# Part of the FFN down products by seven sub-products instead of eight

## The chip, the cores and the metric
One Trainium2 chip, one core. The metric is the device time of one execution in microseconds (us), the median of several runs. Engines: TensorE (PE) multiplies, ScalarE (ACT), VectorE (DVE) and GpSimd (POOL) do elementwise work, SyncE (SP) issues most transfers.

## The reference
Two transformer blocks with four SwiGLU FFNs in all, on 256 tokens of width 1024, in 32-bit floats. Each FFN computes

```
x = x + 0.5 * ((silu(h @ w_gate) * (h @ w_up)) @ w_down)     h = rmsnorm(x)
```

with a hidden width of 2816. `w_down` is 2816 x 1024. The change touches only the product with `w_down`; the rest (mixing layers, attention, norms) is as it was.

## The kernel before
Every product is made from three matmuls on values rounded to the engine's fast 32-bit form: both operands are split in a high part (rounded) and a low part (what is left), and high x high, high x low and low x high are added up in PSUM. The hidden values are split once per FFN (`hid_hi`, `hid_lo`: 22 row blocks of 128, by 256 tokens). The weights are split on the fly, granule by granule.

A granule is a 1 MB piece of weights (4 row blocks of 128 by 512 columns, here called weight blocks; a small one has 2). It goes through a ring of four slots (RING = 4), in three buffers of four slots each: `raw`, `whi`, `wlo`. For granule number g:

- SP loads it into `raw` (`load`, L275) once the low part of granule g - 4 has been made;
- ScalarE makes the high part (`split_hi`, L311), once it is loaded and TensorE has finished granule g - 4;
- VectorE (first granule of a unit) or GpSimd (second granule) makes the low part (`split_lo`, L316);
- TensorE waits for the low part and multiplies (`multiply`, `triple`, L335 to L337), then raises `gran_done`.

A unit is two granules. Each engine works through a program written out by hand, in order; an instruction that waits holds all behind it on that engine. The ring is counted through the whole kernel, so the next stage's first granules are split while the last ones of this stage are multiplied.

In the down stage of an FFN there are six units: for each half of the 1024 output columns three units, with 22 row blocks: granules of 4, 4, 4, 4, 4 and 2. Each granule serves both blocks of 128 tokens: 4 x 2 x 3 = 24 matmuls of 512 columns for a full one. The front half goes to one pair of PSUM banks, the back half to the other pair. VectorE adds each half to x, scaled by half of the token's reciprocal norm (`residual`, L471), and for the front half TensorE transposes the new x in between (`transpose_x`, L416). In the last FFN the last unit is multiplied token block by token block (`multiply_by_token`), so that the end of the kernel can begin sooner.

Before it, in the up stage, 11 units are worked through in the same ring (a loop of three turns over units 3 to 8, `TURNS`). For each piece of 128 hidden columns ScalarE evacuates a part (`low`, L661), VectorE joins (L775), scales and multiplies, ScalarE rounds (L672) and VectorE makes the rest (L789); GpSimd has one split per unit only.

## Time and profile before

| | us |
|---|---|
| median of 3 runs | 1344.33 (1344.03 to 1344.72) |
| span of the profiled execution, first to last instruction | 1343.3 |
| TensorE busy | 1335.2 |
| ScalarE busy | 759.8 |
| VectorE busy | 721.2 |
| GpSimd busy | 536.3 |

The profiled execution is given by its span; the runs are timed around it, and their median stands 1.0 us above the span. Busy time counts the records of an engine. Matmul records overlap, as the engine is pipelined: the price of a matmul on the path is the distance between two starts, not the length of its record. The mean granted TensorE clock was 0.999 of full speed.

### The profile page before, as it was taken

The page shows a single profiled execution, that of the slowest core. Times are in us where ns is not written, and L with a number is a line of the kernel's source. Part 1 is how long each engine was busy: PE and PEld are TensorE (multiplying, and loading weights), DVE is VectorE, ACT ScalarE, POOL GpSimd, SP SyncE. Part 2 cuts the span into 40 slices and gives each one's busy share as a digit, 9 for nine tenths or more (in the row PEclk, how much of TensorE's full clock was granted, in tenths as well). Part 3 has the DMA queues.
Part 4 walks back from the last instruction along what each step waited for, and adds up shares of the span by engine and source line. Part 5 has one row for each costly group of instructions (what it writes and reads, how often), then busy time and mean ns, then how long its engine had stood idle before and what let it go on. Part 6 is the DMA issues. An engine that isn't in the chain of part 4 may idle for free.

```text
span 1343.3 us, 18749 instructions
## 1 busy us (share of the span) xinstructions
PE 1335.2 (99%) x7360; PEld 1128.6 (84%) x7360; DVE 721.2 (54%) x978; ACT 759.8 (57%) x1059; POOL 536.3 (40%) x188
## 2 busy tenths in 40 slices
PE   9999999999999999999999999999999999999998
PEld 8888888888888888888888887788888888888887
DVE  6655346955555444555346659754335642555534
ACT  7655357456555446555347687667434655655533
POOL 1444343474544345444344331035525524444433
PEclk9999999999999999999999999999999999999999
DMA  9656454234655545555454655355855543655550
GB/s 340 226 188 228 172 188 157 96 111 157 212 190 190 207 162 190 197 188 175 173 188 160 240 169 192 122 183 168 300 170 179 177 168 126 208 183 187 188 188 32
DMA packets 38809, 244.32 MB, mean 182 GB/s; under 512 B 5936, under 2 KB 6480, under 8 KB 10832
## 3 DMA queue, kind: packets, MB, share of 16 engines
q1 hardware_dynamic: 36832, 235.08, 51.0%
q10 hardware_dynamic: 1904, 8.23, 1.7%
q8 instruction: 50, 0.82, 0.2%
q14 instruction: 23, 0.19, 0.0%
HBM read 242.21 MB, written 1.08 MB: 181 GB/s over the span
## 4 chain that ended last, share of the span: by engine, by line
PE 96%; DVE 1%; ACT 1%; DMA 1%; issue 0%; SPq 0%; POOLq 0%; POOL 0%; DVEq 0%; ACTq 0%
PE acc L350 21%; PE acc L335 17%; PE acc L337 16%; PE acc L336 16%; PE acc L351 12%; PE acc L353 3%; PE acc L2655 2%; PE work L1006 1%; PE acc L2656 1%; DMA raw<-in_t_ffn_up 1%; PE work L1091 1%; PE work L416 1%; PE work L1097 1%; DVE conv_out L1040 1%; PE work L1940 1%; PE work L2702 1%
## 5 line engine op out<-in xcount | busy, mean ns | idle before, releaser
L316 POOL TENSOR_TENSOR wlo<-raw,whi 128x2048 fp32r<-128x2048 f32 (+1 forms) x104 | 478.5, 4602 | 626.2 <-ACT whi L311 618.3
L311 ACT ACTIVATE whi<-raw 128x2048 fp32r<-128x2048 f32 (+1 forms) x221 | 414.4, 1885 | 98.6 <-PE acc L337 95.6
L350 PE MATMUL acc<-xT,whi 128*128 128x512 f32 x1208 | 427.9, 396 | 0.2 <-DVE work L775 0.2
L316 DVE TENSOR_TENSOR wlo<-raw,whi 128x2048 fp32r<-128x2048 f32 x117 | 298.7, 2553 | 211.9 <-ACT whi L311 211.6
L351 PE MATMUL acc<-xT,wlo 128*128 128x256 f32 x1384 | 373.7, 280 | 0.0
L350 PEld LDWEIGHTS acc<-xT,whi 128*128 128x128 f32 x1208 | 226.6, 188 | 51.0 <-DVE xT L455 0.9
L351 PEld LDWEIGHTS acc<-xT,wlo 128*128 128x128 f32 x1384 | 261.3, 189 | 7.3
L335 PE MATMUL acc<-whi,xT 128*128 128x512 f32 x416 | 168.4, 405 | 0.0
L337 PE MATMUL acc<-whi,xT 128*128 128x512 f32 x416 | 162.5, 391 | 0.0
L336 PE MATMUL acc<-wlo,xT 128*128 128x512 f32 x416 | 162.4, 390 | 0.0
L335 PE MATMUL acc<-whi,hid_hi 128*128 128x512 f32 (+1 forms) x358 | 138.3, 386 | 0.0
L337 PE MATMUL acc<-whi,hid_lo 128*128 128x512 f32 (+1 forms) x358 | 138.1, 386 | 0.0
L336 PE MATMUL acc<-wlo,hid_hi 128*128 128x512 f32 (+1 forms) x358 | 138.0, 386 | 0.0
L775 DVE TENSOR_TENSOR work<-acc,low_parts 128x512 f32<-128x512 f32 x88 | 61.6, 699 | 106.4 <-ACT low_parts L661 105.8
L661 ACT ACTIVATE low_parts<-acc 128x512 f32<-128x512 f32 x88 | 52.6, 598 | 94.2 <-PE acc L353 93.4
L335 PEld LDWEIGHTS acc<-whi,xT 128*128 128x128 f32 x416 | 78.1, 188 | 17.1 <-DVE xT L455 0.7
L337 PEld LDWEIGHTS acc<-whi,xT 128*128 128x128 f32 x416 | 78.1, 188 | 16.8
L336 PEld LDWEIGHTS acc<-wlo,xT 128*128 128x128 f32 x416 | 78.3, 188 | 14.7 <-issue 0.2
L337 PEld LDWEIGHTS acc<-whi,hid_lo 128*128 128x128 f32 x358 | 67.2, 188 | 13.5
L336 PEld LDWEIGHTS acc<-wlo,hid_hi 128*128 128x128 f32 x358 | 67.3, 188 | 13.4
L335 PEld LDWEIGHTS acc<-whi,hid_hi 128*128 128x128 f32 x358 | 67.3, 188 | 13.3
L428 ACT ACTIVATE junk<-x 128x512 bf16<-128x512 f32 (+1 forms) x33 | 20.4, 617 | 93.3 <-DVE x L471 76.1
(402 smaller groups left out, 1617.8 us busy)
## 6 DMA issues: line engine op xcount, KB each, us to landing
raw<-in_t_ffn_up SPq DMA_DIRECT2D x85, 1024.0 KB, 5.0
raw<-in_t_m_in SPq DMA_DIRECT2D x52, 1024.0 KB, 4.9
raw<-in_t_ffn_down SPq DMA_DIRECT2D x40, 1024.0 KB, 4.9
raw<-in_t_m_os SPq DMA_DIRECT2D x8, 1024.0 KB, 5.2
raw<-in_t_ffn_down SPq DMA_DIRECT2D x8, 512.0 KB, 3.5
raw<-in_t_m_out SPq DMA_DIRECT2D x4, 1024.0 KB, 4.9
sum_rows<-row_scratch ACTq DMA_DIRECT2D x4, 1024.0 KB, 4.8
raw<-in_t_m_oa SPq DMA_DIRECT2D x4, 1024.0 KB, 5.1
```

Source lines behind the costliest of these rows:

```text
L311: act.activation(granule(whi, u, i), granule(raw, u, i), ACT.Copy).then_inc(hi_ready, 1)
L316: eng.tensor_tensor(granule(wlo, u, i), granule(raw, u, i), granule(whi, u, i).bitcast(F32), ALU.subtract).then_inc(lo_odd if g % 2 else l ...
L335: pe.matmul(to, xhi[:, kt, tok], hi, start=first, stop=False)
L336: pe.matmul(to, xhi[:, kt, tok], lo, start=False, stop=False)
L337: return pe.matmul(to, xlo[:, kt, tok], hi, start=False, stop=last)
L350: pe.matmul(to, hi[:, c], both_parts(kt), start=first, stop=False)
L351: mm = pe.matmul(to[:, 0:T], lo[:, c], xT_hi[:, kt, :], start=False, stop=False)
L353: mm = pe.matmul(to, hi[:, c], both_parts(kt), start=False, stop=True)
L428: act.activation(junk[:, 0:src.shape[-1]], src, ACT.Square, accum_out=total).then_inc(squares, 1)
L661: act.activation(low_parts[m % 2][:, :, :], acc[:, 2 * q:2 * q + 2, T:2 * T], ACT.Copy).then_inc(ffn_low, 1)
L775: dve.tensor_tensor(work[:, m % 4, :].rearrange("p (a t) -> p a t", a=2), acc[:, 2 * q:2 * q + 2, 0:T], low_parts[m % 2][:, :, :], ALU.add ...
L2655: pe.matmul(banks[blk], hi[:, kt, c], both, start=kt == 0, stop=False)
```

## The change
Of the 22 row blocks of hidden values, the first eight are no longer multiplied directly. Let A be these hidden values, cut into A(token block, row half), each 128 tokens by 512, and B the weights, cut into B(row half, column half), each 512 by 512. Instead of the eight products A x B, seven products of sums are made (Winograd's form of Strassen's method). Each is 4 weight blocks x 3 = 12 matmuls of 512 columns and serves one token block.

- **Sums of tokens.** GpSimd joins high and low part of the eight blocks into `forms` (one 2048-wide addition), then forms the four sums in place with four 512-wide instructions, each waiting for the one before, ahead of its split for the last up unit. ScalarE rounds all of it (`form_hi`), GpSimd makes the rest (`form_lo`, two instructions).
- **Sums of weights.** They are made in the ring's raw slots. A slot that has been split keeps its values, and a transfer issued by GpSimd adds the next block to it in place (`accum_op=ALU.add`). Granules 4, 8 and 12 build on slot 0 one after the other, granule 6 on slot 2. Each such issue waits for the low part of the granule four back. The other 12 granules are loaded by SP as before.
- **Order.** 16 granules in eight units instead of 12 in six: the list `DOWN`. Seven of them are the products P1 to P7, nine the direct granules of the last 14 row blocks.
- **Adding up.** P3 and P5 accumulate in a direct sum's bank. The others get a bank of their own, and VectorE adds each to x once or twice, with the factor or its negative: 14 additions per FFN instead of 4. TensorE waits for some of them (`products_added`) before it takes a bank again.
- **Small things.** A negated scale is made on ScalarE. Several semaphores that were used once are merged into counted ones; the instructions on both sides stay where they were.

The core of the diff:

```diff
+KTS = [(0, 1, 2, 3), (4, 5, 6, 7), (8, 9, 10, 11), (12, 13, 14, 15), (16, 17, 18, 19), (20, 21)]
+DOWN = [(KTS[1], 1, "P4"), (KTS[2], 0, None), (KTS[0], 0, "P6"), (KTS[3], 0, None),
+        (KTS[1], 0, "P3"), (KTS[4], 0, None), (KTS[1], 0, "P7"), (KTS[5], 0, None),
+        (KTS[0], 0, "P1"), (KTS[0], 1, "P2"), (KTS[2], 1, None), ((12, 13), 1, None),
+        (KTS[0], 1, "P5"), ((14, 15), 1, None), (KTS[4], 1, None), (KTS[5], 1, None)]
+ADDED_TO_SLOT = [n for n, (_, _, product) in enumerate(DOWN) if product in ("P3", "P7", "P1", "P5")]
...
-        for half in range(2):
-            add(f"ffn{f}.down{half}.0")
-            add(f"ffn{f}.down{half}.1", [(8, 9, 10, 11), (12, 13, 14, 15)])
-            add(f"ffn{f}.down{half}.2", [(16, 17, 18, 19), (20, 21)])
+        for j in range(len(DOWN) // 2):
+            add(f"ffn{f}.down{j}", [kts for kts, _, _ in DOWN[2 * j:2 * j + 2]])
...
+    forms = cell("forms", 14, [P, KD, T])
+    form_hi = cell("form_hi", 19, [P, KD, T], F32R)
+    form_lo = [cell(f"form_lo{j}", n, [P, 4, T], F32R) for j, n in enumerate((16, 22))]
...
+        so_far = sum(1 for n in added if n <= g and n % RING == g % RING)
+        if g in added:
+            act.wait_ge(added_to_slot[g % RING], 16 * so_far)
+        else:
+            wait(act, raw_ready[g % RING], 16 * (g // RING + 1 - so_far), it, 16)
...
+        for n, (kts, half, product) in enumerate(DOWN):
+            if n not in ADDED_TO_SLOT:
+                load(sp, units[f"ffn{f}.down{n // 2}"], n % 2, down_tiles[half])
...
+    def form_operands(product):
+        i, j, summed = {"P4": (0, 1, False), "P6": (1, 1, True), "P3": (0, 1, True), "P7": (1, 1, False),
+                        "P1": (0, 0, True), "P2": (0, 0, False), "P5": (1, 0, True)}[product]
+        tok, kts = slice(i * P, (i + 1) * P), slice(4 * j, 4 * j + 4)
+        if summed:
+            return form_hi[:, kts, tok], form_lo[j][:, :, tok]
+        return hid_hi[:, kts, tok], hid_lo[:, kts, tok]
+
+    FRONT_BANKS, BACK_OF_X = pair(0), pair(0)
+    PRODUCT_BANK = {"P4": acc[:, 2, :], "P6": acc[:, 3, :], "P3": acc[:, 0, :], "P7": work[:, 2, :],
+                    "P1": work[:, 3, :], "P2": work[:, 2, :], "P5": acc[:, 1, :]}
+
+    def down_done(f, n):
+        return units[f"ffn{f}.down0"].g + n + 1
+
+    def multiply_form(pe, u, i, product):
+        wait_lo(pe, u.g + i)
+        hi, lo = granule(whi, u, i), granule(wlo, u, i)
+        ahi, alo = form_operands(product)
+        bank, shared = PRODUCT_BANK[product], product in ("P3", "P5")
+        for j in range(4):
+            pe.matmul(bank, ahi[:, j, :], hi[:, j, :], start=j == 0 and not shared, stop=False)
+            pe.matmul(bank, ahi[:, j, :], lo[:, j, :], start=False, stop=False)
+            mm = pe.matmul(bank, alo[:, j, :], hi[:, j, :], start=False, stop=j == 3 and not shared)
+        mm.then_inc(gran_done, 1)
...
+        hidden_needed = {0: 8, 1: 12, 3: 16, 5: 20, 7: 22}
+        for n, (kts, half, product) in enumerate(DOWN):
+            u, i = units[f"ffn{f}.down{n // 2}"], n % 2
+            if n in (0, 1):
+                pe.wait_ge(joined, PIECES * f + 21 + n)
+            if n in hidden_needed:
+                pe.wait_ge(hidlo_done, PIECES * f + hidden_needed[n])
+            if product == "P6":
+                pe.wait_ge(forms_made, 3 * (f + 1))
+            if product == "P2":
+                pe.wait_ge(products_added, 2 * f + 1)
+            if n == 10:
+                pe.wait_ge(products_added, 2 * f + 2)
+            if product is not None:
+                multiply_form(pe, u, i, product)
+            elif f == 3 and n >= 14:
+                if n == 14:
+                    multiply_by_token(pe, u, hid_hi, hid_lo, BACK_OF_X, ffn_banks(NCH)[0][:, 0:256])
+            else:
+                multiply(pe, u, i, hid_hi, hid_lo, pair(0), n in (1, 10), n in (7, 15))
+            if n == 10 and b + 1 != B_OUT:
+                transpose_x(pe, b + 1, 0)
...
+        act.wait_ge(forms_made, 3 * f + 1)
+        act.activation(form_hi[:, :, :], forms[:, :, :], ACT.Copy).then_inc(forms_rounded, 1)
...
+        last_added = {}
+
+        def add_to_x(t, half, bank, alpha, signal=None, value=None):
+            c = slice(half * 512, (half + 1) * 512)
+            if (t, half) in last_added:
+                dve.wait_ge(*last_added[t, half])
+            op = dve.scalar_tensor_tensor(out=x[:, t, c], in0=bank, scalar=alpha[t], in1=x[:, t, c],
+                                          op0=ALU.mult, op1=ALU.add)
+            if signal is None:
+                last_added[t, half] = S["dve_chain"], dlink(op)
+            else:
+                op.then_inc(signal, 1)
+                last_added[t, half] = signal, value
+
         step(10, None, lambda: split_lo(dve, down[0], 0))
         step(11, None, lambda: split_lo(dve, down[1], 0))
         split_lo(dve, down[2], 0)
+        if b + 1 == B_MIX2:
+            dve.wait_ge(x_rescaled, NT)
+        dve.wait_ge(sq_done, 2 * (b + 1))
+        dve.wait_ge(gran_done, down_done(f, 0))
+        add_to_x(0, 0, PRODUCT_BANK["P4"], MINUS_HALF_RSTD)
+        add_to_x(0, 1, PRODUCT_BANK["P4"], HALF_RSTD)
         split_lo(dve, down[3], 0)
-        residual(dve, b + 1, 0, down[2], ffn_banks(NCH), HALF_RSTD)
+        dve.wait_ge(gran_done, down_done(f, 2))
+        add_to_x(0, 0, PRODUCT_BANK["P6"], HALF_RSTD)
+        add_to_x(1, 0, PRODUCT_BANK["P6"], MINUS_HALF_RSTD)
+        split_lo(dve, down[4], 0)
+        dve.wait_ge(gran_done, down_done(f, 6))
+        add_to_x(1, 0, PRODUCT_BANK["P7"], HALF_RSTD)
+        add_to_x(1, 1, PRODUCT_BANK["P7"], MINUS_HALF_RSTD, products_added, 2 * f + 1)
+        split_lo(dve, down[5], 0)
+        dve.wait_ge(gran_done, down_done(f, 8))
+        add_to_x(0, 0, FRONT_BANKS[0], HALF_RSTD)
+        add_to_x(1, 0, FRONT_BANKS[1], HALF_RSTD, products_added, 2 * f + 2)
+        add_to_x(0, 0, PRODUCT_BANK["P1"], HALF_RSTD, resid_done, 2 * b + 1)
         if b + 1 == B_FFN2:
             apply_final1(dve, 0)
-        split_lo(dve, down[4], 0)
+        split_lo(dve, down[6], 0)
+        add_to_x(1, 1, PRODUCT_BANK["P1"], MINUS_HALF_RSTD)
+        dve.wait_ge(gran_done, down_done(f, 9))
+        add_to_x(0, 1, PRODUCT_BANK["P2"], HALF_RSTD)
+        add_to_x(1, 1, PRODUCT_BANK["P2"], MINUS_HALF_RSTD)
+        split_lo(dve, down[7], 0)
         if b == B_FFN0:
             dve.wait_ge(params_loaded, 16 * len(PARAMS))
         if b + 1 != B_OUT:
             rest_xt(dve, b + 1, 0)
-        for u in down[5:]:
+        for u in next_units:
             split_lo(dve, u, 0)
+        for t in range(NT):
...
+        down, tiles = [units[f"ffn{f}.down{j}"] for j in range(len(DOWN) // 2)], w[f"t_ffn{f}_down"]
+
+        def add_to_slot(n):
+            kts, half, _ = DOWN[n]
+            g = down[0].g + n
+            wait_lo(pool, g - RING)
+            pool.dma_start(raw[:, g % RING, :], tiles[half][:, kts[0] * KT:(kts[-1] + 1) * KT],
+                           accum_op=ALU.add).then_inc(added_to_slot[g % RING], 16)
+
+        def block_of(i, j):
+            return forms[:, 4 * j:4 * j + 4, i * P:(i + 1) * P]
+
+        def form(to, other, op):
+            link(pool, pool.tensor_tensor(block_of(*to), block_of(*to), block_of(*other), op))
+
+        pool.wait_ge(hidlo_done, PIECES * f + 8)
+        if b == B_FFN2:
+            pool.wait_ge(x_rescaled, NT)
+        link(pool, pool.tensor_tensor(forms[:, :, :], hid_hi[:, 0:KD, :].bitcast(F32), hid_lo[:, 0:KD, :].bitcast(F32),
+                                      ALU.add))
+        form((1, 1), (1, 0), ALU.subtract)
+        form((1, 0), (0, 0), ALU.add)
+        form((0, 0), (1, 1), ALU.subtract)
+        form((0, 1), (0, 0), ALU.subtract)
+        pool.sem_inc(forms_made, 1)
         step(9)
-        for half in range(2):
-            for j in range(3):
-                split_lo(pool, units[f"ffn{f}.down{half}.{j}"], 1)
+        for j in range(2):
+            pool.wait_ge(forms_rounded, f + 1)
+            kts = slice(4 * j, 4 * j + 4)
+            pool.tensor_tensor(form_lo[j][:, :, :], forms[:, kts, :], form_hi[:, kts, :].bitcast(F32),
+                               ALU.subtract).then_inc(forms_made, 1)
+        split_lo(pool, down[0], 1)
+        add_to_slot(4)
+        split_lo(pool, down[1], 1)
+        add_to_slot(6)
+        add_to_slot(8)
+        split_lo(pool, down[2], 1)
+        split_lo(pool, down[3], 1)
+        add_to_slot(12)
+        for j in (4, 5, 6, 7):
+            split_lo(pool, down[j], 1)
```

## Rows read from the trace of the kernel before

**Rows 1.** The page, busy time, share of the span and instructions of each engine.
```profile
PE 1335.2 (99%) x7360; PEld 1128.6 (84%) x7360; DVE 721.2 (54%) x978; ACT 759.8 (57%) x1059; POOL 536.3 (40%) x188
```

**Rows 2.** The page, chain of work that ended last, shares by engine.
```profile
PE 96%; DVE 1%; ACT 1%; DMA 1%; issue 0%; SPq 0%; POOLq 0%; POOL 0%; DVEq 0%; ACTq 0%
```

**Rows 3.** Groups by line and shape: busy us, mean ns | idle before, releasers.
```profile
L316 POOL TENSOR_TENSOR wlo<-raw,whi 128x2048 fp32r<-128x2048 f32 x96 | 451.5, 4704 | 614.4 <-ACT whi L311 606.5 <-DVE invT L1613 7.9
...
L311 ACT ACTIVATE whi<-raw 128x2048 fp32r<-128x2048 f32 x213 | 405.9, 1916 | 81.4 <-PE acc L337 78.6 <-ACT junk L428 1.9 <-ACT ba L1399 0.2
...
L316 DVE TENSOR_TENSOR wlo<-raw,whi 128x2048 fp32r<-128x2048 f32 x117 | 298.7, 2553 | 211.9 <-ACT whi L311 211.6 <-DVE k_tok L1556 0.2
...
L335 PE MATMUL acc<-whi,hid_hi 128*128 128x512 f32 x346 | 134.9, 390 | 0.0
```

**Rows 4.** Order of time, TensorE, first FFN's down stage: start us, us.
```profile
131.62 0.39 PE L335 MATMUL acc<-whi,hid_hi 128*128 128x512 f32 x1
...
166.99 1.04 PE L416 MATMUL work<-ident,x 128*128 128x128 f32 x8
...
192.39 0.39 PE L335 MATMUL acc<-whi,xT 128*128 128x512 f32 x1
```

**Rows 5.** Busy time by engine, granted clock, DMA share in the first down stage.
```profile
core 0: us, PE busy (x) PEld busy (x) DVE busy (x) ACT busy (x) POOL busy (x), PEclk, DMA share, GB/s
131.60:191.50 59.90, 59.90 (x270) 49.64 (x269) 23.05 (x16) 25.10 (x23) 25.28 (x6) 1.00 0.53 192
```

**Rows 6.** Order of time, GpSimd, end of first FFN's up stage, start of down.
```profile
102.77 4.66 POOL L316 TENSOR_TENSOR wlo<-raw,whi 128x2048 fp32r<-128x2048 f32 x1 [6.47 <-ACT whi L311]
113.97 4.65 POOL L316 TENSOR_TENSOR wlo<-raw,whi 128x2048 fp32r<-128x2048 f32 x1 [6.54 <-ACT whi L311]
...
136.37 4.67 POOL L316 TENSOR_TENSOR wlo<-raw,whi 128x2048 fp32r<-128x2048 f32 x1 [6.55 <-ACT whi L311]
143.91 2.40 POOL L316 TENSOR_TENSOR wlo<-raw,whi 128x1024 fp32r<-128x1024 f32 x1 [2.87 <-ACT whi L311]
```

**Rows 7.** Order of time, ScalarE, same stretch.
```profile
117.69 0.39 ACT L672 ACTIVATE hid_hi<-work 128x256 fp32r<-128x256 f32 x1 [0.50 <-DVE work L784]
120.61 0.60 ACT L661 ACTIVATE low_parts<-acc 128x512 f32<-128x512 f32 x1 [2.54 <-PE acc L353]
...
134.37 1.92 ACT L311 ACTIVATE whi<-raw 128x2048 fp32r<-128x2048 f32 x1
...
137.33 1.92 ACT L311 ACTIVATE whi<-raw 128x2048 fp32r<-128x2048 f32 x1
```

**Rows 8.** Order of time, VectorE, first FFN, then a row of the last.
```profile
111.85 2.29 DVE L316 TENSOR_TENSOR wlo<-raw,whi 128x2048 fp32r<-128x2048 f32 x1 [0.64 <-ACT whi L311]
...
139.27 3.91 DVE L316 TENSOR_TENSOR wlo<-raw,whi 128x2048 fp32r<-128x2048 f32 x1 [1.51 <-ACT whi L311]
...
161.75 1.41 DVE L471 SCALAR_TENSOR_TENSOR x<-acc,half_rstd,x 128x512 f32<-128x512 f32 x2 [9.30 <-PE acc L337]
...
1316.12 5.32 DVE L316 TENSOR_TENSOR wlo<-raw,whi 128x2048 fp32r<-128x2048 f32 x1 [1.31 <-ACT whi L311]
```

**Rows 9.** DMA issues: KB each, median us to landing; SP's issues, ns min/median/max.
```profile
raw<-in_t_ffn_down SPq DMA_DIRECT2D x40, 1024.0 KB, 4.9
...
raw<-in_t_ffn_down SPq DMA_DIRECT2D x8, 512.0 KB, 3.5
...
raw<-in_t_ffn_up SPq DMA_DIRECT2D x4, 512.0 KB, 7.4
...
L275 SPq DMA_DIRECT2D raw<-in_t_ffn_down x48: 327/328/430, 105.4 to 1306.0; - x48
...
DMA to landing us min/median/max: 3.4/4.9/6.9
```

**Rows 10.** Order of time, GpSimd, last FFN's down stage.
```profile
1314.36 4.93 POOL L316 TENSOR_TENSOR wlo<-raw,whi 128x2048 fp32r<-128x2048 f32 x1 [8.41 <-ACT whi L311]
1319.54 4.14 POOL L316 TENSOR_TENSOR wlo<-raw,whi 128x1024 fp32r<-128x1024 f32 x1 [0.26 <-ACT whi L311]
```

102 lines of the change are left out of this document (48 added, 54 removed).

## The prediction
> **What bounds the kernel now.** I read the busy times first. TensorE is busy 1335.2 of 1343.3 us and no other engine passes 57% [rows 1]; the chain that ended last is 96% TensorE [rows 2]. So only fewer TensorE instructions, or a stall put into its stream, can move the end. Next, the order of time on TensorE in the first FFN's down stage. The first product starts at 131.62 and the transposes begin at 166.99 behind 132 + 24 = 156 matmuls, so one 512-column matmul costs 35.37 / 156 = 0.2267 us of the path, though its row says 389 ns (the records overlap) [rows 3, 4]. The stage has 264 of them and ends at 192.39: 59.85 us of matmuls and 0.8 us of transposes, no idle time. Taking 0.389 for the price would overrate the change by 1.7.
>
> Then I read what feeds TensorE there. Over 131.6:191.5 ScalarE is busy 25.1 of 59.9 us, VectorE 23.1, GpSimd 25.3, DMA 53% [rows 5]. There is room on average; the question is latency. The ring has four slots: a granule's high part can be made only when TensorE has finished the granule four back, its low part only after that.
>
> **What goes away.** Seven products of 12 matmuls take the place of 8 x 12 for the first eight row blocks: 264 becomes 252 per FFN. Four FFNs save 48 x 0.2267 = 10.9 us. That is the ceiling, 0.8% of the time. The last 14 row blocks, the transposes and the by-token split at the end keep their counts.
>
> **What is added, and what hides it.** Per FFN, granules rise from 12 to 16 and weight blocks split from 44 to 56.
> - ScalarE: 3 more full granules and one pass over the forms, 4 x 1.92 = 7.7 us [rows 3, 7], and a 0.2 us scale. 25.1 becomes 33 of 57: hidden, unless order delays it.
> - VectorE: two more splits at 2.29 us and ten more additions to x at 0.705 (two took 1.41) [rows 8]: 11.6 us. 23.1 becomes 35 of 57.
> - GpSimd: one more granule 4.65; the forms, one 2048-wide addition 4.65 and four 512-wide ones, at 2.40 / 1024 per element [rows 6] about 1.2 each; two 1024-wide rests 2.4 each; four DMA issues. About 19 us more, 14 of it before the down stage.
> - DMA: 10 MB plain and 4 MB accumulating instead of 11 MB plain.
>
> The forms start when GpSimd has finished the last split of the Fori loop, at 107.43 (102.77 + 4.66), where it idled until 113.97 [rows 6]. The big addition ends at 112.1, VectorE's split takes 2.29, the four small ones end near 119.3. ScalarE waits for them from 118.1 (117.69 + 0.39), rounds until 121.2 and reaches its next evacuation 0.6 us later than 120.61 [rows 7]; TensorE needs that only at 126.1, so this is free. GpSimd's split of up10 moves from 113.97 to 119.3 and ends at 124.0, due at 126.1: free, with 2 us left. The two rests end at 128.8 and the split of granule 1 at 133.4.
>
> **The down stage, in time after its start E = 131.6.** With 0.2267 per matmul an undisturbed TensorE starts granules 0 to 15 at 0, 2.7, 8.2, 10.9, 16.3, 19.0, 24.5, 27.2, 29.9, 32.6, 35.4, 41.6, 44.3, 47.0, 49.8, 55.2. Half of them are now 2.72 us long where every full one was 5.44, so four slots cover much less time. Two costs are not in the trace:
> - Landing time of a 1 MB accumulating transfer. Plain ones land in 4.9 us, 512 KB in 3.5 [rows 9]: 1.4 per 512 KB, so 2.1 fixed and 2.8 moving. The accumulate reads its destination as well, so it can't be shorter than 4.9; with both reads moved it is 2.1 + 5.6 = 7.7. Plain loads are in flight beside it (granule 5 beside the first, granule 7 beside the second), so I take 8.4. The far end is two slow plain transfers in a row, 2 x 6.9 = 13.8 [rows 9]. I take the value near the doubled one, as the read side is all that doubles.
> - What an issue holds GpSimd. SP's take 0.33 [rows 9]; the upper end is one GpSimd split, 4.65. I take 1.0, nearer to SP's row.
>
> A price that only pages have: the Trainium skill (DMA: Bandwidth & Descriptors, "Anatomy of one DMA — SWDGE (gpsimd) path") fits 2.0 us and bytes over 436 GB/s for a GpSimd transfer, and (Collectives: The Full Stack, "The bandwidth ceiling: the fold count and why AG ≠ RS ≠ AR") holds that an add in the DMA path costs through its second source read. As an estimate that makes 2.0 + 2 x 2.4 = 6.8 us for 1 MB, and the sum would be the full 10.9.
>
> Also, two engines cannot split at once. In the last FFN a VectorE split began at 1316.12 and lasted 5.32 us; GpSimd's ended at 1319.29, and 1319.29 + 2.29 is 1321.6 [rows 8, 10]. In the first, one began at 139.27, GpSimd's ended at 141.04, and VectorE's lasted 3.91 [rows 6, 8]. So where both are wanted I let VectorE wait. The Trainium skill (SBUF — State Buffer, "Who interferes with whom") has this as a lock: a VectorE instruction with two SBUF inputs shuts out a GpSimd one that reads SBUF. By that rule more GpSimd work costs VectorE too, which speaks against this change; the rows agree.
>
> Now the chain. Granule 1's low part is ready at 1.8, due 2.7. GpSimd issues the sum for granule 4 at 1.8; it lands at 10.2. High part 12.1, low part (VectorE) 14.4, due 16.3: fine. But GpSimd's next item is the issue for granule 8, which waits for granule 4's low part, and behind it stands granule 5's low part: issue until 15.4, split until 20.0, due 19.0. **Stall 1.0 us.** This wait did not exist before. Granule 6: issued at 9.4 behind granule 3's split (136.37 + 4.67 is E + 9.4 [rows 6]), landed 17.8, high 19.7, VectorE waits for GpSimd until 20.0, low 22.3, due now 25.5. Granule 7's low part is ready at 24.7, due 28.2. Granule 8: issued 14.4, landed 22.8, high 24.7, low 27.0, due 30.9. Granule 9: the issue for 12 holds GpSimd until 28.0, low 32.6, due 33.6. Granule 10: VectorE blocked until 32.6, low 34.9; then two additions free the front banks at 36.4, due 36.4. Granule 12: landed near 35.4, ready by 42, due 45. Behind that every split has 3 us or more, and the residual and the transposes have their operands as early as before.
>
> Sum per FFN: -2.72 + 1.0, and 0.1 for waits that only touch: -1.6. Four: -6.4 us. The profiled execution goes from 1343.3 to 1336.9; the median of the runs stands 1.0 above that span, so I forecast **1337.9 us**.
>
> How steep this is: landing at 7.7 or less gives no stall, 1333.4 (full 10.9). At 9 us granule 5 is 1.6 late and the front banks 0.6: 2.2 of 2.72 are gone, 1342. Break-even is at 9.3 us.
>
> **Rivals.**
> 1. *The accumulating transfers are slow and the ring runs dry* (slower). Place: granule 4's sum, then granule 5 behind the issue for 8, then 8, 9 and 10. It decides from a landing time of 9.3 us. For it: four transfers per FFN each wait for a split and each hold the next split; and in the kernel's first microseconds, with many loads in flight at once, 512 KB took 7.4 us to land instead of 3.5 [rows 9]. Against: DMA is 53% busy in the stage [rows 5]. At 13.8 us: granule 4's low part is ready at 19.8 (3.5 late), granule 5's at 25.4 (2.9 more), 8's at 37.8 (1.5), 9's at 43.4 (2.9), and the front banks at 47.2 (1.0): 11.8 late, 9.1 net per FFN, +36 us, 1380. At 11.5 us the same steps lose 1.2 + 2.9 + 0 + 2.1 + 1.0 = 7.2, 4.5 net, +18 us, 1362.
> 2. *All hidden* (faster by more): landing at 7.7 or less and issues of 0.4 us. TensorE stays without idle time: 1333.4.
> 3. *GpSimd's own time decides*, issues of 2 us or more with good landings: granules 5 and 9 each come about 1 us later per extra us, so 2 us takes back another 1.0 + 0.7 per FFN and leaves nothing: 1344, at most 1350.
> 4. *The saving is not there*, because the matmuls of a product run at another pace than those of before: same width, same number of weight loads, the same 0.2267 pitch is expected. Little chance.
>
> **Chances.** Forecast case (landing 7.8 to 8.9): 0.37, own range 1334 to 1341. All hidden: 0.20. Slow transfers: 0.28. GpSimd's time: 0.12. Other, the fourth among it: 0.03. About 0.2% (2.7 us) can be told from no change, so faster means below 1341.6: 0.37 + 0.20 + 0.01 of the other = 0.58. Within: half of the third and the near edge of the first rival, 0.12. Slower: 0.30. The lower end of the range is the full saving with 1 us to spare, 1332.5; the upper, with some 0.15 left out of the slow case, 1365.
>
> **What would show it.** Right: 48 matmuls fewer in all (7360 instructions on TensorE become 7312), a pitch of 0.2267 within a product, TensorE idle of about 1 us in each down stage, ended by GpSimd's low part of granule 5; accumulating transfers landing in 8 to 9 us; VectorE splits of 4 to 5 us beside GpSimd's. Wrong: waits of TensorE for granules 4, 8, 9 or 10, ScalarE waiting for a DMA before its high parts of 4, 6 or 8 (rival 1), or no idle time at all (rival 2). If the down stages take 57.9 us each, and the end has not moved by 10 us, my account of the stages around it is wrong.

## The result, and the profile after

The changed kernel takes 1370.47 us (median of 4 runs, 1364.18 to 1374.1) against 1344.36 beside it: ratio 1.019, 95% interval 1.0164 to 1.0215. It is slower. 1337.9 was forecast, with 1334 to 1341 for its own case; it went the way of the first rival, between the two times worked out for it (1362 and 1380).

The profiled execution is the longest of the four (1374.1 us); its span is 1372.3, 29.0 more than before, and the split of the loss below is for it. The page of the changed kernel, busy times and the shares of the chain that ended last, answers to [rows 1, 2]:

```profile
PE 1333.9 (97%) x7312; PEld 1121.8 (82%) x7312; DVE 783.2 (57%) x1026; ACT 791.6 (58%) x1083; POOL 643.2 (47%) x240
...
PE 52%; issue 21%; POOL 16%; DMA 5%; ACT 3%; DVE 3%; POOLq 0%; SPq 0%; ACTq 0%; DVEq 0%
```

The 48 matmuls are gone (7360 to 7312). But TensorE holds only 52% of the chain where it held 96%: GpSimd (16%), the DMA (5%) and time in which an engine waited for nothing that the profile shows ("issue", 21%) are on it now. What TensorE waited for, in its waits (us in total, times, longest):

```profile
PE acc L353 <- POOL wlo L334: 16.2, 8, 2.9
...
PE acc L353 <- DVE x L914: 8.2, 3, 2.7
PE acc L609 <- DVE wlo L334: 4.8, 4, 1.8
```

GpSimd's low parts are there eight times, granules 1 and 5 of each FFN; VectorE's additions to x stand ahead of granule 10 three times, VectorE's low part ahead of granule 4 four times. The first FFN's down stage as a window (length; busy us of PE, PEld, DVE, ACT, POOL; granted clock; DMA share; GB/s), and three stretches of 5 us in it:

```profile
131.10:199.80 68.70, 60.77 (x262) 48.78 (x261) 39.33 (x28) 30.83 (x27) 36.51 (x13) 0.98 0.80 231
156.00:161.00 5.00, 5.00 (x22) 4.14 (x23) 5.00 (x3) 1.92 (x1) 2.13 (x1) 1.00 0.82 267
171.00:176.00 5.00, 2.26 (x10) 1.58 (x9) 5.00 (x4) 1.91 (x1) 1.10 (x1) 0.92 0.56 157
176.00:181.00 5.00, 5.00 (x18) 3.99 (x18) 4.41 (x5) 2.50 (x5) 1.94 (x1) 0.74 0.86 331
```

The stage is 68.7 us long, before 60.8. The four stages are 68.7, 67.6, 67.5 and 68.3, before 60.8, 60.8, 60.7 and 60.2: 29.5 us more in all, which is the whole difference of the spans. The starts of TensorE's matmuls split that into 10.9 us saved, about 32.5 us of standing still and about 7.3 us of matmuls further apart than 0.227 us behind a standstill. Net 28.9. Most of the 7.3 us are matmuls at 0.43 us, and they don't follow every standstill. TensorE sat idle for 2.7 to 2.9 us seven times. Behind three of them, 6 to 14 matmuls came at 0.43 us; in the first stage the granted clock fell from 1.0 to 0.74 over 176:181, TensorE being at its level of 1.2 GHz for part of that stretch. Behind the other four the spacing was 0.227 us again from the second or third matmul on and the clock stayed at 1.00, as in 156:161.

In the first stage, TensorE's timeline shows four of the standstills (start, duration; in brackets the idle time and what ended it):

```profile
135.21 0.47 PE L353 MATMUL acc<-whi,hid_hi 128*128 128x512 f32 x1 [1.22 <-POOL wlo L334]
...
150.09 0.50 PE L609 MATMUL acc<-whi,form_hi 128*128 128x512 f32 x1 [1.03 <-DVE wlo L334]
...
155.94 0.47 PE L353 MATMUL acc<-whi,hid_hi 128*128 128x512 f32 x1 [2.83 <-POOL wlo L334]
...
175.63 0.79 PE L353 MATMUL acc<-whi,hid_hi 128*128 128x512 f32 x1 [2.74 <-DVE x L914]
```

They stand ahead of granules 1, 4, 5 and 10. From start to start they cost 1.4, 1.2, 3.0 and 2.9 us; the other stages show the same list within 0.8 us, but for the second, which has none ahead of granule 10. Ahead of granule 9 three stages lose another 0.2 to 0.5 us.

GpSimd's timeline of the same stretch:

```profile
111.57 7.34 POOL L994 TENSOR_TENSOR forms<-forms 128x512 f32<-128x512 f32 x4
119.09 4.64 POOL L334 TENSOR_TENSOR wlo<-raw,whi 128x2048 fp32r<-128x2048 f32 x1 [0.18 <-POOL forms L994]
123.68 6.83 POOL L1010 TENSOR_TENSOR form_lo<-forms,form_hi 128x1024 fp32r<-128x1024 f32 x2
130.48 4.59 POOL L334 TENSOR_TENSOR wlo<-raw,whi 128x2048 fp32r<-128x2048 f32 x1
135.02 1.04 POOL L987 DMA_DIRECT2D raw<-in_t_ffn_down  x1
...
150.34 0.86 POOL L987 DMA_DIRECT2D raw<-in_t_ffn_down  x1 [7.83 <-DVE wlo L334]
150.90 7.23 POOL L334 TENSOR_TENSOR wlo<-raw,whi 128x2048 fp32r<-128x2048 f32 x2
```

Up to 123.7 this is within 0.2 us of the forecast (the whole trace runs 0.5 us ahead of the one before: 102.25 for 102.77). The two rests take 6.83 us instead of 4.8, so granule 1's low part ends at 135.0, 4.0 after the stage's start and not 1.8, and the first sum is issued there. VectorE had begun a split just before:

```profile
123.23 2.65 DVE L334 TENSOR_TENSOR wlo<-raw,whi 128x2048 fp32r<-128x2048 f32 x1 [0.64 <-ACT whi L329]
```

It ends at 125.88, 2.2 us after the rests began; 2.2 and two rests of 2.4 are 7.0. The landing times (the DMA view: issuer, count, size, median us; then minimum, median and maximum of GpSimd's 16):

```profile
raw<-in_t_ffn_down SPq DMA_DIRECT2D x32, 1024.0 KB, 5.0
raw<-in_t_ffn_down POOLq DMA_DIRECT2D x16, 1024.0 KB, 9.8
```

```profile
DMA to landing us min/median/max: 7.9/9.8/11.5
```

The four of this stage, issued at 135.0, 141.6, 150.3 and 164.2, landed in 10.8, 10.3, 8.0 and 8.6 us. Beside each of the first two SP issued a plain load 0.1 us later (1 MB beside the first, 512 KB beside the second), and the two sums overlap each other by 4.1 us. The third is overlapped for 1.6 us, the fourth not at all, and the next plain load started 5.5 us behind them. An issue holds GpSimd for 0.88. And VectorE's splits, beside GpSimd's pairs of splits at 150.90 and 164.80:

```profile
147.75 2.29 DVE L334 TENSOR_TENSOR wlo<-raw,whi 128x2048 fp32r<-128x2048 f32 x1 [9.31 <-ACT whi L329]
...
153.86 6.43 DVE L334 TENSOR_TENSOR wlo<-raw,whi 128x2048 fp32r<-128x2048 f32 x1 [2.50 <-ACT whi L329]
...
167.60 6.66 DVE L334 TENSOR_TENSOR wlo<-raw,whi 128x2048 fp32r<-128x2048 f32 x1 [1.80 <-ACT whi L329]
```

Alone a split takes 2.29. The one at 153.86 came while GpSimd worked on the first of a pair and ended 2.2 us after the end of the second (150.90 + 7.23 = 158.13; 158.13 + 2.29 = 160.42): it let both pass. Six of the eight such splits in the four stages took 6.4 to 7.1 us, the other two 4.1 and 3.3.

### The profile page after: what moved, and what is told of

Same layout as the page of the kernel before. It is cut to its first block, busy times and chain, and to the rows that moved or that the text cites. A ratio compares the mean times of both kernels' runs of the same rounds, so it can differ in the third digit from the quotient of the medians.

```text
span 1372.3 us, 18846 instructions
## 1 busy us (share of the span) xinstructions
PE 1333.9 (97%) x7312; PEld 1121.8 (82%) x7312; DVE 783.2 (57%) x1026; ACT 791.6 (58%) x1083; POOL 643.2 (47%) x240
## 4 chain that ended last, share of the span: by engine, by line
PE 52%; issue 21%; POOL 16%; DMA 5%; ACT 3%; DVE 3%; POOLq 0%; SPq 0%; ACTq 0%; DVEq 0%
PE acc L353 13%; PE acc L355 12%; PE acc L354 12%; POOL wlo L334 10%; DMA raw<-in_t_ffn_down 4%; POOL forms L994 2%; POOL form_lo L1010 2%; ACT whi L329 2%; PE acc L2790 2%; DVE wlo L334 2%; POOL forms L999 1%; PE acc L368 1%; PE work L1141 1%; PE acc L2791 1%; PE work L434 1%
## 5 line engine op out<-in xcount | busy, mean ns | idle before, releaser
L334 POOL TENSOR_TENSOR wlo<-raw,whi 128x2048 fp32r<-128x2048 f32 (+1 forms) x112 | 499.8, 4484 | 496.9 <-ACT whi L329 488.3
L329 ACT ACTIVATE whi<-raw 128x2048 fp32r<-128x2048 f32 (+1 forms) x237 | 437.5, 1857 | 132.6 <-DMA raw<-in_t_ffn_down 78.4
L334 DVE TENSOR_TENSOR wlo<-raw,whi 128x2048 fp32r<-128x2048 f32 x125 | 334.8, 2678 | 225.7 <-ACT whi L329 225.4
L368 PE MATMUL acc<-xT,whi 128*128 128x512 f32 x1208 | 427.8, 396 | 0.0
L353 PE MATMUL acc<-whi,hid_hi 128*128 128x512 f32 (+1 forms) x230 | 92.2, 401 | 24.4 <-POOL wlo L334 16.2
L355 PEld LDWEIGHTS acc<-whi,xT 128*128 128x128 f32 x416 | 78.1, 188 | 16.8
L354 PE MATMUL acc<-wlo,hid_hi 128*128 128x512 f32 (+1 forms) x230 | 90.4, 393 | 0.0
L354 PEld LDWEIGHTS acc<-wlo,xT 128*128 128x128 f32 x416 | 78.3, 188 | 14.7 <-issue 0.2
L355 PE MATMUL acc<-whi,hid_lo 128*128 128x512 f32 (+1 forms) x230 | 90.3, 392 | 0.0
L353 PEld LDWEIGHTS acc<-whi,hid_hi 128*128 128x128 f32 x230 | 44.7, 194 | 37.3 <-issue 19.3
L720 ACT ACTIVATE gate_act<-work 128x256 f32<-128x256 f32 x88 | 33.2, 380 | 57.5 <-DVE work L836 57.5
L845 DVE TENSOR_TENSOR hid_lo<-work,hid_hi 128x256 f32 (+1 forms) x88 | 37.3, 424 | 50.5 <-ACT hid_hi L724 50.0
L371 PE MATMUL acc<-xT,whi 128*128 128x512 f32 x176 | 65.7, 396 | 0.0
```

The lines of the kernel that those rows point to most:

```text
L329: act.activation(granule(whi, u, i), granule(raw, u, i), ACT.Copy).then_inc(hi_ready, 1)
L334: eng.tensor_tensor(granule(wlo, u, i), granule(raw, u, i), granule(whi, u, i).bitcast(F32), ALU.subtract).then_inc(lo_odd if g % 2 else l ...
L353: pe.matmul(to, xhi[:, kt, tok], hi, start=first, stop=False)
L354: pe.matmul(to, xhi[:, kt, tok], lo, start=False, stop=False)
L355: return pe.matmul(to, xlo[:, kt, tok], hi, start=False, stop=last)
L368: pe.matmul(to, hi[:, c], both_parts(kt), start=first, stop=False)
```

## The experiments

The theories in the expectations: T, the accumulating transfers land too late; G, GpSimd comes too late or in the wrong order; W, the waits on GpSimd's stream do it by themselves; L, GpSimd's back-to-back splits hold VectorE up; S, the spacing of the accumulating transfers; C, the order of the granules; Q, an issue and its wait in GpSimd's queue delay the split behind them. Kernels of one comparison ran beside the kernel before, whose median stayed within 1344.16 to 1344.51. The changed kernel's own runs lie 10 us apart, so a difference of 2 or 3 us between it and a version of it says little.

**The same transfers without the adding.** Leaves out the weight sums.

```diff
-                           accum_op=ALU.add).then_inc(added_to_slot[g % RING], 16)
+                           ).then_inc(added_to_slot[g % RING], 16)
```

> Leaves out the adding of the weight sums: GpSimd issues the same four transfers per FFN at the same places, but as plain copies, so granules 4, 6, 8 and 12 hold one weight block instead of a sum. Changed kernel 1370.5, before 1344.4. Theory T (the accumulating transfers land too late, 9.8 us in the profile): a plain 1 MB transfer lands in 5 to 6.5, so about 4 us come off at granules 4/5 and 8/9/10 of each FFN; the 1.4 us stall at granule 1 stays. 1370.5 - 4 x (4 to 6) = 1346 to 1355. Theory G (GpSimd is late before any transfer is issued, because the token sums take 19 us and not 14): the stall at granule 1 stays and most of those at 5 and 10, 1362 to 1370.

1358.57 us, ratio 1.0096 (1.0081 to 1.0112): between the two. They land in 6.2 instead of 9.8, an issue takes 0.58. Granule 1's stall is as it was (1.38), so is the one at granule 10 in three FFNs; granule 4's is gone and 5's is 0.7 to 2.0. Adding accounts for 12 of the 26 us lost. The stall at granule 10 follows the lock here, with the data early. The timeline of the second FFN, whose granule 10 starts at 491.92, 2.73 us idle, behind these and the additions to x:

```profile
481.42 6.97 POOL L334 TENSOR_TENSOR wlo<-raw,whi 128x2048 fp32r<-128x2048 f32 x2
483.61 6.94 DVE L334 TENSOR_TENSOR wlo<-raw,whi 128x2048 fp32r<-128x2048 f32 x1 [1.35 <-ACT whi L329]
```

**All sixteen loads on SP's queue**, GpSimd neither issues nor waits. Leaves out the weight sums.

```diff
-ADDED_TO_SLOT = [n for n, (_, _, product) in enumerate(DOWN) if product in ("P3", "P7", "P1", "P5")]
+ADDED_TO_SLOT = []
...
-        add_to_slot(4)
...
```

> Leaves out the adding of the weight sums: all 16 granules are plain loads from SP in order, GpSimd issues nothing. Theory T: as with the plain copies from GpSimd or 2 to 4 us per FFN better, because no issue (0.9 us) and no wait for VectorE's low part stands ahead of granule 5's and 9's splits on GpSimd any more: 1340 to 1348. Theory G: 1355 to 1368, the token sums still delay granules 1 and 3.

1339.45, ratio 0.9962 (0.9948 to 0.9976), at the edge of what T gave. Only granule 1's stall is left, 4.9 us in four FFNs. The added granules, splits, forms and additions to x are hidden otherwise.

**The same loads, but GpSimd keeps its four waits.** Leaves out the weight sums. `ADDED_TO_SLOT` is empty here too.

```diff
-            pool.dma_start(raw[:, g % RING, :], ...
-                           accum_op=ALU.add).then_inc(added_to_slot[g % RING], 16)
```

> As the run with 16 plain loads from SP (1339.5; leaves out the adding of the weight sums), but GpSimd keeps the four waits for the low part of the granule four back, at the places of its issues, without issuing anything. It parts the wait in GpSimd's queue from the transfer. Theory W (the wait for granule 4's low part standing ahead of granule 5's split is a cost of its own, whatever lands): granule 5's low part comes 4.6 us after VectorE's of granule 4, 1350 or more. Theory T (only late data makes it cost): with plain loads granule 4's low part is early, so the waits are over when GpSimd gets there or within 1 us: 1339 to 1342.

1339.72, ratio 0.9965 (0.9953 to 0.9978), equal to the one above. Where the data come early the waits cost nothing: W falls.

**No token sums, no rounding of them, no rests.** Leaves those out.

> Leaves out the sums of tokens (five GpSimd additions, ScalarE's rounding, GpSimd's two rests per FFN): the products use the unsummed hidden values, everything else as in the changed kernel, accumulating transfers too. GpSimd's split of granule 1 is back at E - 1.8 and the first sum is issued 5 to 6 us earlier. Theory G: no stall at granules 1, 4 and 5, at most 1 to 2 us at 9/10: 1337 to 1342. Theory T: the transfers still land in 9.8 us, stalls at 8, 9, 10 stay: 1350 to 1362.

1356.51, ratio 1.0088 (1.0074 to 1.0103), as T had it. The stalls at granules 1 and 4 go, but with GpSimd 14 us freer at the start they only move to granules 9 and 10 (7.3 us idle for GpSimd's low parts, 7.0 for VectorE's additions). GpSimd's load ahead of the stage is a part, not the cause.

This run also parts the plain load from the second sum. The first sum of each FFN is issued 1.9 us before the stage and SP's 1 MB load 0.1 us behind it, and no other sum is in flight but for 0.3 us in the second FFN. Its landing took 10.7, 11.5, 10.8 and 10.6 us. The first FFN's, with the SP issue and GpSimd's landing:

```profile
129.35 1.04 POOL L981 DMA_DIRECT2D raw<-in_t_ffn_down  x1
129.44 0.33 SPq L289 DMA_DIRECT2D raw<-in_t_ffn_down  x1
DMA to landing us min/median/max: 10.7/10.7/10.7
```

**Only the order of the rests**: the one that P1 needs goes behind the issue for granule 6.

```diff
-        for j in range(2):
+        form_rest(1)
         split_lo(pool, down[0], 1)
...
         add_to_slot(6)
+        form_rest(0)
```

> Nothing left out. Only the order on GpSimd: the rests of the token sums of the first row half (needed by P1 and P5 alone, from granule 8 on) are made after the issue for granule 6 instead of before granule 1's split; TensorE waits for them at P1. Takes 3.4 us out of GpSimd's stream ahead of granule 1. By my reading of the trace both theories let it win: the stall at 1 goes (1.4), those at 4 and 5 shrink from 4.2 to about 1: 4 x 4 = 16 us, 1352 to 1358 under T and G alike; under T the rest (granule 10, 2.9 and the slower clock behind it) stays. If the time is within 5 us of 1370, the chain through granule 1 is not what holds.

1362.17, ratio 1.012 (1.0094 to 1.0146). Granule 1's stall is gone, 8.3 us are back, 2.8 more than granule 1's share (4 x 1.37), which the spread of the runs doesn't tell from nothing. The one at granule 5 stays at 2.99, so I missed by 4 or more: granule 4's low part releases TensorE, which has 2.72 us of product from it, and GpSimd, which first issues (its split starts 0.6 later) and then splits for 4.6 to 4.9 before granule 5 is ready. In all four FFNs of this run and of the changed kernel this leaves a gap of 3 us, though granule 4 was 0 to 1.9 late.

**Only the lock**: GpSimd lets VectorE's low part go ahead.

```diff
+        wait_lo(pool, down[0].g + 6)
         split_lo(pool, down[3], 1)
         add_to_slot(12)
-        for j in (4, 5, 6, 7):
+        split_lo(pool, down[4], 1)
+        wait_lo(pool, down[0].g + 10)
+        for j in (5, 6, 7):
```

> Nothing left out. The changed kernel with two more waits on GpSimd: its split of granule 7 waits for VectorE's of granule 6, and that of 11 for VectorE's of 10. In the changed kernel GpSimd runs 5 and 7 (9 and 11) back to back and VectorE's split between them takes 6.4 to 6.7 us, as it gets SBUF only after both. Theory L (this lock is a part of the loss): granule 10's low part and the front additions come 2.4 us earlier, so the 2.9 us stall at granule 10 and the slower clock behind it (1.8 us) shrink: 4 x 2.5 to 4 x 4.5, 1352 to 1360. Theory T alone: VectorE's splits are not what is late, granule 10 waits for its data: 1368 to 1372.

1362.1, ratio 1.0129 (1.0112 to 1.0146): 8.4 us less than the changed kernel, 2 us above the range of L, and the stall at granule 10 gone. VectorE's splits of 6.4 to 7.1 us are down to 4.4 or less. L holds for that stall.

**The first sum issued first**, ahead of GpSimd's splits of granules 1 and 3, with the rest that P1 needs behind the split of granule 5; alone, and with the two waits. The issues for 6 and 8 stay behind granule 3's split.

```diff
+        form_rest(1)
+        add_to_slot(4)
         split_lo(pool, down[0], 1)
-        add_to_slot(4)
         split_lo(pool, down[1], 1)
```

> Nothing left out. Order on GpSimd: rest of the second row half, issue for granule 4, split of 1, split of 3, issue for 6, issue for 8, split of 5, rest of the first row half, split of 7, and on. The first accumulating transfer is issued 7 us earlier than in the changed kernel (E - 3 instead of E + 4) and before SP's load of granule 5. With 10 us to land, granule 4's low part is ready at about E + 11.5, due at E + 16.3: no stall at 4 and 5 under T, 1338 to 1345, if stalls at 9 and 10 vanish with it. Theory L: those at 10 stay (2.9 + 1.8 per FFN), 1348 to 1356.

> Nothing left out. The two waits for VectorE together with the new order. Under T and L together nothing is left but what touches: 1344.5 - 10.9 and at most 1 us per FFN, 1334 to 1339. If it is not under 1341, a third cause is open.

1360.06 and 1350.65 (ratios 1.0114, 1.0097 to 1.0131; and 1.0053, 1.0036 to 1.0071). Both missed: 1348 to 1356 was the upper range for the first, 1334 to 1339 for the second. The stalls at 1, 4 and 5 are gone. With the waits one of more than 0.8 us is left in each FFN, which I had not expected:

```profile
PE work L609 <- POOL wlo L334: 9.8, 4, 2.9
```

That is granule 9, whose split stands behind the issue for 12. This issue waits for VectorE's low part of granule 8, and the sum for 8 took 12.8 to 14.5 us to land: it was issued 2.5 us behind the one for 6.

**That order with plain copies.** Leaves out the weight sums.

> Leaves out the adding of the weight sums: the order of the version at 1350.7, with plain copies from GpSimd (6.2 us to land) in place of accumulating ones (8.7 to 10). Theory T: what remains at granule 9 is late data, so all stalls go: 1344.3 - 10.9 and at most 0.5 per FFN, 1333.5 to 1336. Theory Q: the issues stay in the queue, but with granule 8 early they don't wait, the same. If 1340 or more remains, neither landing nor the waits explain the stall at granule 9.

1333.87, ratio 0.9923 (0.9907 to 0.994), landing 6.3. No stall; stages of 58.1 us. This is the full saving (1333.4 in the prediction), so the matmuls give what was reckoned, and at equal order the adding alone costs 1350.65 - 1333.87 = 16.8 us. GpSimd's first transfer of each FFN has the same place in both, with no other of GpSimd's in flight: plain it lands in 5.1 to 5.3 us, adding in 8.0 to 8.1.

**Granule 9's split ahead of the issue for 12; and then the front sums in banks of their own as well.**

> Nothing left out. The order of the last version (1350.7) and GpSimd's split of granule 9 ahead of its issue for granule 12, which waits for VectorE's low part of granule 8. Theory Q (an issue and its wait in GpSimd's queue delay the split behind it): granule 9 comes 1.4 us earlier, TensorE's stall there falls from 2.2 to 3.0 us to about 1.2 and the stretch at the slower clock behind it gets shorter: 4 x 1.5 to 2.5 us, 1341 to 1345. Theory T only (granule 9 waits for its data, as granule 8's sum lands 13 us after its issue): within 2 us of 1350.7.

> Nothing left out. As the run before it, and the direct front sums go to the other pair of banks (P4 and P6 to two work banks), so TensorE begins granule 10 without waiting for VectorE's additions of the front sums. If the wait for these additions still costs (0.4 to 1.3 us per FFN in the traces), 1338 to 1342; if granule 10 then waits for its own low part instead, the same time as the run before it.

1359.2 and 1361.81 (ratios 1.0116 and 1.0128): both worse than 1350.65, and both missed. Granule 9's stall falls from 2.2 to 3.0 us to 0.7 to 1.7, but the sum for 12 is issued 4 us later and the stall moves there, 2.6 to 3.8 us. This sum now also goes out 0.1 us ahead of a plain load, with two more 2.2 and 4.7 us behind it, and lands in 10.6 to 11.9 us with no other sum in flight; in the version at 1350.65 it took 7.9 to 8.0. The first one's waits:

```profile
PE acc L609 <- DVE wlo L334: 11.2, 4, 3.3
...
PE work L609 <- POOL wlo L334: 4.0, 4, 1.5
```

**Each accumulating transfer in two halves.**

```diff
+            for h in range(2):
+                pool.dma_start(raw[:, g % RING, h * 2 * KT:(h + 1) * 2 * KT], tiles[half][:, at:at + 2 * KT],
+                               accum_op=ALU.add).then_inc(added_to_slot[g % RING], 16)
```

> Nothing left out. The changed kernel with each accumulating transfer cut in two of 512 KB, issued one after the other. Measures the transfer. If the second read is what makes it long (fixed part about 2 to 3 us, 6 to 7 us of moving per 1 MB), a half lands in about 6 us when alone and the pair in 10 to 11; if the cost is per transfer (GpSimd's path), each half takes 8 or more and the pair 12 or more. GpSimd holds 0.9 us twice. Time 1370 to 1380.

1401.63 in a single run, far outside. A half lands in 5.4 to 6.1 by itself, and the two halves of the first sum are in 11 to 12 us after the issue, no sooner than one whole transfer. But GpSimd stood ahead of an issue with nothing in the profile that it waited for; its timeline:

```profile
141.72 0.88 POOL L989 DMA_DIRECT2D raw<-in_t_ffn_down  x1
146.28 0.89 POOL L989 DMA_DIRECT2D raw<-in_t_ffn_down  x1 [3.68 <-issue]
...
152.36 0.86 POOL L989 DMA_DIRECT2D raw<-in_t_ffn_down  x1 [0.91 <-issue]
...
172.42 0.88 POOL L989 DMA_DIRECT2D raw<-in_t_ffn_down  x1 [5.49 <-issue]
```

Each time it is the second half of a pair that was held back, in every pair of this stage but the first; with one transfer per sum the changed kernel's issues have only VectorE's low parts ahead of them. What holds it the run doesn't show.

**Spread**: the four sums about 8 us apart or more. It starts from the version at 1350.65 (first sum first, two waits). The granules go in another order (a full back granule is number 7, a plain one stands between P1 and P2), the front sums have banks of their own, the issue for 6 stands ahead of granule 3's split, the second rest behind the issue for 12.

```diff
-        (KTS[1], 0, "P3"), (KTS[4], 0, None), (KTS[1], 0, "P7"), (KTS[5], 0, None),
-        (KTS[0], 0, "P1"), (KTS[0], 1, "P2"), (KTS[2], 1, None), ((12, 13), 1, None),
-        (KTS[0], 1, "P5"), ((14, 15), 1, None), (KTS[4], 1, None), (KTS[5], 1, None)]
+        (KTS[1], 0, "P3"), (KTS[4], 0, None), (KTS[1], 0, "P7"), (KTS[2], 1, None),
+        (KTS[0], 0, "P1"), (KTS[5], 0, None), (KTS[0], 1, "P2"), (KTS[3], 1, None),
+        (KTS[0], 1, "P5"), ((16, 17), 1, None), ((18, 19), 1, None), (KTS[5], 1, None)]
```

> Nothing left out. Theory C (the chain through ring slot 0): granules 0, 4, 8 and 12 share one slot, each sum can be issued only when the one before it is split, so a link is 10 us to land + 1.9 high + 2.3 low + 0.4 = 14.6 at least, and TensorE leaves 13.6 us between granules 4 and 8 and 14.4 between 8 and 12; the order of work on GpSimd can only say which link stalls. This version spreads the links: a full back granule as 7, a full one as 11, the small one of the front as 9, P2 as 10, front sums in banks of their own, so TensorE leaves 16.3, 16.3 and 13.6 us (46.2 in all to granule 12). Under C almost nothing is left to wait for: 1344.2 - 10.9 + at most 1 per FFN, 1334 to 1339. If only GpSimd's order and the lock were at fault (1350.7 was what they gave back), this is no better than 1348.

> Nothing left out. As v_spread with GpSimd's issue for granule 6 behind its split of granule 3 instead of ahead of it. Granule 3 is due 10.9 us after the start and has 0.5 us of room in v_spread; granule 6's sum comes 4.6 us later here, which should still do (due 24.5). Within 2 us of v_spread; if granule 3 was late there, 1 us per FFN better here.

The first: 1335.4 us, ratio 0.9935 (0.9921 to 0.9948). **It computes everything and beats both kernels**: 9 us below the one before, 35 below the changed one. Its page:

```profile
PE 1323.9 (99%) x7306; PEld 1117.8 (84%) x7306; DVE 796.3 (60%) x1026; ACT 791.9 (59%) x1083; POOL 645.6 (48%) x240
...
PE 97%; DVE 1%; ACT 1%; issue 0%; DMA 0%; POOLq 0%; POOL 0%; DVEq 0%; ACTq 0%
```

VectorE, ScalarE and GpSimd are as busy as in the changed kernel, but none of them has more than 1% of the chain. (7306 matmuls and not 7312, as the unit that is multiplied token block by token block at the end is smaller in this order.) Its sums are issued and land so:

```profile
128.11 1.05 POOL L990 DMA_DIRECT2D raw<-in_t_ffn_down  x1
...
136.37 0.89 POOL L990 DMA_DIRECT2D raw<-in_t_ffn_down  x1 [2.52 <-DVE wlo L334]
...
144.37 0.88 POOL L990 DMA_DIRECT2D raw<-in_t_ffn_down  x1 [2.46 <-DVE wlo L334]
```

```profile
DMA to landing us min/median/max: 7.9/8.1/10.0
```

An issue ahead of GpSimd's own split has another effect. SP's load for the next slot is released by the end of that split; in the changed kernel it therefore went out 0.1 us behind the sum, here it goes 5.6 us behind it.

The second differs only in the issue for 6, which stands behind granule 3's split as in the changed kernel. I expected it within 2 us of the first; it took 1348.35, ratio 1.0031 (1.0019 to 1.0043). In the first stage the sum of 6 goes out 4.1 us later, 0.1 us ahead of a 1 MB plain load and 2.5 us ahead of the sum of 8, and the two land in 10.8 and 14.1 us:

```profile
140.50 0.89 POOL L990 DMA_DIRECT2D raw<-in_t_ffn_down  x1
...
143.00 0.86 POOL L990 DMA_DIRECT2D raw<-in_t_ffn_down  x1 [1.62 <-DVE wlo L334]
...
155.65 4.61 POOL L334 TENSOR_TENSOR wlo<-raw,whi 128x2048 fp32r<-128x2048 f32 x1 [7.15 <-DVE wlo L334]
```

```profile
DMA to landing us min/median/max: 10.8/12.4/14.1
```

In all four FFNs the first of the pair took 10.6 to 11.0 us and the later 13.9 to 14.7. In the version before it, where the sums hardly overlap, the same two took 8.0 to 8.2 and 8.2 to 8.8 but for one of 10.0. For the later one the plain loads next to it start as before (2.4 us ahead, 5.5 us behind), so there it is the other sum that costs 4 to 6 us: S holds for the landing. For the first of the pair it isn't shown, as a plain load at the same moment gives 10.6 to 10.8 alone.

The 13 us between the two versions are not the landings alone. TensorE stalls ahead of granule 7 (1.7 to 1.8 us) and granule 11 (0.9). Granule 7 is the split at 155.65: GpSimd's added wait holds it for VectorE's low part of granule 6, 7.15 us here. That part is late by the later issue (4.1) and by the longer landing (2.8). As an estimate from these rows, with a landing of 8.0 granule 7 would have been ready about 1 us before TensorE needed it, so both were needed. The second version without the two waits was not run.

**What of the spread version is the granules' order, what the two waits.**

> Nothing left out. GpSimd's order of v_spread (1335.4) with the granules in the order of the changed kernel (front sums in banks of their own). It parts two readings of v_spread. Theory C (the chain through slot 0 needs TensorE work between its links): 13.6 and 14.4 us are left again instead of 16.3 and 13.6, so 1 to 2.5 us of stall per FFN come back at granule 9 or 12: 1338 to 1345. Theory S (what counts is that the accumulating transfers are not in flight two at a time; in v_spread they are 8 us apart and land in 8.1, in v_spread_b two were 2.5 us apart and landed in 11 and 14): issues are as far apart as in v_spread, within 2 us of 1335.4.

> Nothing left out. v_spread without the two waits that let VectorE split granules 6 and 10 before GpSimd goes on. Theory L (GpSimd's splits back to back shut VectorE out): VectorE's split of 6 or 10 lasts 6 us or more and stalls of 1 to 3 us come back: 1339 to 1348. If the time stays within 2 us of 1335.4, there is room enough for the lock once the transfers are early.

With the old order of granules 1338.92, ratio 0.9959 (0.9944 to 0.9973): granule 9 stalls for about 1 us per FFN, so C is worth 3.5 us, within C's range. (The two differ in one more place: with the old order the second rest stands ahead of the issue for 12, not behind it. That issue went out at the same time in both, 28.2 and 28.3 us after the start in the first FFN.) Without the waits 1335.11, ratio 0.9935 (0.9919 to 0.9952): once each split has a few us to spare the lock costs nothing, though it cost 8.4 us in the changed kernel.

## Why the prediction was wrong

Much of it stood. The saving is 48 matmuls at 0.2267 (the plain order reaches 1333.9, forecast 1333.4 for that). The forms are ready when reckoned. The place where the ring would run dry was named, granule 5 behind the issue for 8. An issue costs 0.88 (1.0 taken). The steps that failed:

1. **"so I take 8.4"** for the landing. The way to it was right for one transfer by itself: twice the reads gave 7.7, the runs show 7.9 to 8.2 where nothing else starts beside it. But it was one number for all. With a plain load issued at the same moment and a second sum overlapping by 4 us or more it is 10.3 to 11.5 (the first two sums of each FFN), and 13.9 to 14.7 for the later of two sums 2.5 us apart. In the first stage granule 4's sum took 10.8, 2.4 more than I took. I had seen that granule 5's plain load flies beside it and allowed 0.7 for that; 8.0 alone and the 2.8 that a plain 1 MB needs to move, from the prediction's own split of [rows 9], make 10.8. The run without token sums bears this out: with that load at the same moment and no second sum it is 10.6 to 10.8 in three FFNs, and 11.5 in the one where another sum overlapped for 0.3 us.
2. **"The two rests end at 128.8 and the split of granule 1 at 133.4"**: 130.5 and 135.0, in a trace that runs 0.5 us ahead. I had let VectorE wait wherever both engines want to split; here GpSimd waited. The Trainium skill (SBUF — State Buffer, "Who interferes with whom") says that issue order decides who blocks, and the trace has both: 6.83 us for GpSimd's two rests of 2.4 behind VectorE's split of 123.23, and 6.43 for VectorE's split of 2.29 behind GpSimd's. With this, granule 4's low part is ready at 14.4 + 2.4 + 2.2 = 19.0 after the start, as measured, against a due time that granule 1's stall had moved to 17.7. Break-even was 0.9 us above my value and the two errors made 4.6.
3. **"VectorE waits for GpSimd until 20.0, low 22.3"**, and the same for granule 10. It mostly lets a whole pair of splits pass, not the rest of one: 6.4 to 7.1 us. That makes the stall ahead of granule 10, and giving way to VectorE returned 8.4 us.
4. **Not in the sum**: what a stall does to the clock. Behind three of the seven idle times of 2.7 to 2.9 us, 6 to 14 matmuls came at 0.43 us. With the slower first matmul behind each stall that is 7.3 us in four FFNs, about a fifth of the 39.8 us lost. In the rival's sum it was missing too.

Two slips in the working changed nothing. Granule 7 is a small granule, so its split takes 2.4 us and not 4.65. And by the prediction's own chain a landing of 7.7 leaves 0.3 us of stall per FFN; none is left from 7.4 down.

Rival 1 was therefore right in direction and for granules 4, 5 and the front banks ahead of granule 10. It had nothing at granule 1 (1.4 measured), 1.0 at the front banks where 2.9 was measured, and 2.1 at granule 9 where at most 0.5 was. Its times for 11.5 us (1362) and 13.8 us (1380) enclose the result, but that is partly luck: the landing times are 7.9 to 11.5, and late GpSimd, the lock and the clock made up the difference. The range to 1365 left it out because I weighed it at landing times alone.

Shown: adding costs 16.8 us at equal order; the waits by themselves nothing where the data are early; the lock 8.4; order and spacing decide whether the saving comes through. Open: how much of the way from 1350.65 to 1335.4 each placement is worth, since several were changed together and the share of the granules' order, 3.5 us, is from one pair; how much of the 13 us between the two spread versions is the waits' part; and what holds GpSimd ahead of an issue when transfers are halved.

## What to carry to other kernels

Where a ring of few slots gets a producer that reads twice, work out when each of its transfers flies and beside what: a landing time from a row of lone transfers is the lower end. Keep two of the kind from overlapping, and keep other engines' loads from starting at the same moment. A stall can cost more than its own length: the low part that ended it also releases the engine that must make the next one, and TensorE sometimes comes back slower. Write the order of the engine that issues and computes so that issues stand ahead of its own splits, and leave a few us at each; then a lock that cost 8 us in the tight schedule costs nothing, as in the spread version.

## What the hardware showed beyond that

- A 1 MB accumulating transfer lands in 7.9 to 8.2 us with no other sum in flight and no plain load starting within 4 us of it (the first of each FFN in the versions that issue it first). With a plain 1 MB load issued 0.1 us behind it and no other sum it takes 10.6 to 10.8 in three FFNs. As the later of two sums 2.5 us apart it takes 12.7 to 14.7.
- The same transfer from GpSimd without adding lands in 5.1 to 5.3 us with next to nothing beside it and in 6.2 to 6.3 in the median of a run; SP's in 5.0. GpSimd's issue takes 0.88 with adding and 0.58 without.
- Two splits back to back on GpSimd mostly hold a waiting VectorE split of 2.29 us up for both: it then takes 6.4 to 7.1 us in the changed kernel. Behind a single one it took 3.91 [rows 8]. The other way round, GpSimd's two rests of 2.4 us took 6.83 behind one split of VectorE.
- After seven idle times of 2.7 to 2.9 us the matmuls came at 0.43 instead of 0.227 us three times, 6 to 14 of them, with a granted clock of 0.74 over 5 us in one case; four times they didn't, with a clock of 1.00.
- With the accumulating transfers halved, GpSimd stood 3.7, 0.9 and 5.5 us ahead of the second half's issue.
